# Expert weights in 4 MB transfers with 32 KB runs instead of 2 MB halves with 16 KB runs

## The chip, the cores and the metric

The kernel runs on one core of a Trainium2 chip. The metric is the device time of one execution in microseconds (us). Three executions of the kernel before took 2572.22 to 2574.54 us, median 2573.12 us.

## What is computed

The reference runs two blocks one after the other on 512 tokens of 1024 float32 features. The first (a recurrent layer, a pooling layer and their dense feed-forward parts) is not touched by the change. The second has two layers (`l` = 0, 1), each an attention part and then a mixture of experts, cut here to what matters:

```python
aff = jax.nn.softmax(logits, axis=-1)              # 512 tokens x 16 experts
gate, idx = lax.top_k(aff.transpose(0, 2, 1), 64)  # each expert takes 64 tokens
xs = x[bidx, idx]
hid = jax.nn.silu(xs @ w_gate) * (xs @ w_up)       # per expert, 64 x 1024
ys = (hid @ w_down) * gate
return jnp.zeros_like(x).at[bidx, idx].add(ys)
```

`w_gate`, `w_up` and `w_down` are 1024 x 1024 float32 for each of 16 experts, so 4 MB a matrix, 48 matrices or 201 MB a layer.

## The kernel before, in words

Everything is placed by hand in one SBUF array, `arena`, and every engine has its own instruction stream with semaphore waits written out.

**Slots.** The weights of the experts go through a ring of 11 slots of 16 KB per partition (`ring2`, each 2 MB in all). A matrix is loaded as two halves of 512 rows. Partition p of a half holds rows 4p to 4p+3, which are contiguous in memory: one run of 16 KB per partition (`load`, L476 to L499, the transfer itself at L493 for most halves). The halves are numbered n = 0 to 95 in the order of their use. Two experts make a pair: halves 12i to 12i+11 are gate and up of expert 2i, gate and up of expert 2i+1, and then the first halves of both w_down and the second halves of both. Half n goes to slot `ORDER[n % 11]`, so the load of half n waits until half n - 11 was used. The first eleven wait instead for the end of whatever lay in their slot before. Half 11 goes in two pieces (L488, L489). SyncE's queue issues all of these in order, and each load stands behind the wait of the one ahead of it. The last four halves are cut finer: L495 loads their first 8 KB per partition, L503 (`load_rest`) the rest, the very last ones by columns.

**TensorE**, for each expert: `inner` (matmuls at L2711) multiplies the 64 gathered tokens by gate and then by up, 16 matmuls of 512 columns for each half matrix; two column halves of the result run side by side on the two 64-column halves of the array, one for weight columns 0 to 511, one for 512 to 1023. Then four transposes of `hid` (L2790). After the second expert of a pair, `outer` (L2745) multiplies both experts' hidden rows by their two w_down matrices, side by side: first with both first halves, then, after a further wait, with both second halves. Between these lie the matmuls that add the previous pair's result into the tokens (`scattered`, L2756) and the transposes of the next pair's gathered tokens (L2696; for the first two experts L2684). In the last pair `outer_last` (L2729) and `scattered_last` (L2763) do the same in finer steps.

A transposed token chunk must have the rows that the weights have: as partition p holds rows 4p to 4p+3 of a half, the transposes read every fourth feature (L2684, L2696), and the layer's norm gain is brought in the same order (`gperm`).

**GpSimdE** gathers the tokens of each next pair from memory by an indirect transfer (128 rows of 4 KB), issued once the previous gathered tokens have been transposed.

After layer 0 the same SyncE queue goes on with layer 1's input weights (`w_in`, L463), which wait for slots of the ring, and with `w_out` (L511).

Of the kernel before, what the change touches and what calls it, by code (L numbers as in the profile page):

```python
# [19 lines left out]
D = 1024  # L20
# [71 lines left out]
def program(nc, a, out):  # L92
    with ExitStack() as ctx:
# [54 lines left out]

        ring2 = [at(lo, SLOT) for lo in (0, 4096, 8192, 12288, 16384, 20480, 41472, 28672, 45568, 32768, 50176)]
        x_tok = at(24576, 4096, "p (t d) -> p t d", t=TC)  # L150
# [195 lines left out]
        R2_LANDS = (3, 2, 2, 1, 1, 2, 0, 0, 0, 0, 1)  # L346
        ORDER = (10, 2, 1, 4, 3, 8, 7, 5, 0, 6, 9)
        LOADS = 6 * EXPERTS

        def loads_before(s, n):  # L350
            return sum(1 for i in range(n) if ORDER[i % 11] == s)

        def expert_load(l, n):
            s = ORDER[n % 11]
            k = loads_before(s, n)
            total = slot_total(s)
            twice = total - loads_before(s, LOADS)
            late = twice if k else 0
            return s, l * total + k + late, l * total + k + 1 + twice, 16 * (l * (R2_LANDS[s] + total) + R2_LANDS[s] + k + 1 + late)

        def slot_total(s):
            return loads_before(s, LOADS) + (1 if s == ORDER[0] else 0)

        def load_number(e, part):
            i, par = divmod(e, 2)
            return 12 * i + (4 * par + part if part < 4 else 8 + 2 * (part - 4) + par)

        def part_used(l, e, part):
            s, _, done, _ = expert_load(l, load_number(e, part))
            return r2_used[s], done  # L370

        def part_in(l, e, part):
            s, _, _, landed_at = expert_load(l, load_number(e, part))
            return s, landed_at

# [4 lines left out]
        def _(sp):  # L380
# [69 lines left out]
            for l in range(DEPTH):  # L450
# [4 lines left out]
                for s in ((10, 3, 1, 0, 4, 2), (0, 10, 4, 2, 1, 3))[l]:  # L455
                    c0, n = {0: (1152, 416), 1: (0, 384), 2: (384, 384), 3: (768, 384), 4: (1568, 384), 10: (1952, 384)}[s]
                    if l:
                        sp.wait_ge(r2_used[s], slot_total(s))
# [10 lines left out]
                def load(n):  # L469

                    i, j = divmod(n, 12)
                    e, part = (2 * i + j // 4, j % 4) if j < 8 else (2 * i + j % 2, j // 2)
                    s, free, _, _ = expert_load(l, n)
                    if n >= 11:
                        sp.wait_ge(r2_used[s], free - 1 if n == 11 else free)
                    else:  # L476
                        name, value = {10: ("conv_ps", 6 * l + 6), 0: ("wout_ps", 24 * l + 24), 1: ("q_ps", 3 * l + 3), 2: ("p2_ps", 16 * l + 16),
                                       3: ("o_ps", 18 * l + 18), 4: ("sc_done", 12 * l + 12), 5: ("wout_ps", 24 * l + 16),
                                       6: ("lgp_ps", 4 * l + 4), 7: ("wout_ps", 24 * l + 8),
                                       8: ("t_ps", 2 * l + 2), 9: ("xn_saved", 64 * l + 64)}[s]  # L480
                        sp.wait_ge(sm[name], value)
                        if s == 9:
                            sp.wait_ge(got[0], 16 * (8 * l + 1))
                    w = a[("w_gate_2", "w_up_2", "w_down_2")[part // 2]][l, e]
                    half = w[512 * (part % 2):512 * (part % 2) + 512, :]
                    if n == 11:
                        for k in (0, 2):
                            sp.wait_ge(r2_used[s], free - 1 + k // 2)  # L488
                            sp.dma_start(ring2[s].rearrange("p (k n) -> p k n", k=4)[:, k:k + 2],  # L489
                                         half.rearrange("(p k) n -> p k n", k=4)[:, k:k + 2]).then_inc(r2_in[s], 16)  # L490
                        return
                    if n < LOADS - 4:
                        sp.dma_start(ring2[s], half.rearrange("(p k) n -> p (k n)", k=4)).then_inc(r2_in[s], 16)  # L493
                        return
                    sp.dma_start(ring2[s][:, 0:2048].rearrange("p (k n) -> p k n", k=2),  # L495
                                 half.rearrange("(p k) n -> p k n", k=4)[:, 0:2]).then_inc(r2_in[s], 16)

                def load_rest(n, landed, lo, hi):

                    s = expert_load(l, n)[0]  # L500
                    q = (n - LOADS + 4) // 2
                    half = a["w_down_2"][l, EXPERTS - 2 + n % 2][512 * q:512 * q + 512, :]
                    sp.dma_start(ring2[s][:, 2048:].rearrange("p (k n) -> p k n", k=2)[:, :, lo:hi],  # L503
                                 half.rearrange("(p k) n -> p k n", k=4)[:, 2:4, lo:hi]).then_inc(landed, 16)

                if l:
                    sp.wait_ge(r2_used[5], loads_before(5, LOADS))
                else:
                    sp.wait_ge(sm["f2_ps"], F2_BASE[1] + 28)
# [6 lines left out]
                for n in (LOADS - 4, LOADS - 3):  # L516
                    load(n)
                for par in range(2):
                    load_rest(LOADS - 4 + par, r1_in[2 + par], 0, D)
                for n in (LOADS - 2, LOADS - 1):  # L520
                    load(n)
                for par in range(2):
                    load_rest(LOADS - 2 + par, r1_in[par], 0, 512)
                for par in range(2):
                    load_rest(LOADS - 2 + par, last_cols_in[par], 512, D)
            for half in range(2):
# [1393 lines left out]
        def _(pe):  # L1920
# [397 lines left out]
            for l in range(DEPTH):  # L2318
# [42 lines left out]
                def landed(s, n):  # L2361

                    pe.wait_ge(r2_in[s], 16 * (l * (R2_LANDS[s] + slot_total(s)) + n))
                    return ring2[s]
# [311 lines left out]
                def gathered(e):  # L2676
# [4 lines left out]
                    for k in range(KC):  # L2681
                        q, kk = divmod(k, 4)
                        src = xg[e][:, 512 * q:512 * q + 512].rearrange("c (p k) -> c k p", k=4)[:, kk, :]
                        ins = tr(ps[:, 4, CAP * k:CAP * k + CAP], src, ident[CAP * e:CAP * e + CAP, CAP * e:CAP * e + CAP])  # L2684
                    ins.then_inc(sm["xst_ps"], 1)

                def gathered_pair(i, q):
# [6 lines left out]
                    for kk in range(4):  # L2694
                        src = xg_pair[:, 512 * q:512 * q + 512].rearrange("c (p k) -> c k p", k=4)[:, kk, :]
                        ins = tr(ps[:, 4, P * kk:P * kk + P], src, ident)  # L2696
                    ins.then_inc(sm["xst_ps"], 1)

                def piece(e, part):

                    s, landed_at = part_in(l, e, part)
                    pe.wait_ge(r2_in[s], landed_at)
# [102 lines left out]
        def _(pool):  # L2805
# [20 lines left out]
            def second_tables():  # L2826
                for l in range(DEPTH):
# [151 lines left out]
```

## Time and profile before

| | us |
|---|---|
| median of three runs | 2573.12 |
| the profiled execution, its own time | 2574.44 |
| its span in the trace | 2572.6 |
| TensorE busy | 2474.2 (96% of the span) |
| VectorE busy | 1156.5 (45%) |
| SyncE's DMA queue (169072 packets, 544.59 MB) | 54.8% of 16 engines' span |

Times in the trace count from the start of the span. The expert stage of layer 0 lies at 1362.87 to 1807 us (first matmul of expert 0 to the end of L2763), that of layer 1 at 2124.56 to 2569 us. "Idle before" in a row is the time in which the engine did nothing ahead of that row, with what ended it.

### The profile page before, as it was taken

What the parts mean: (1) busy time and instruction counts of PE and PEld (TensorE: products, weight loads), DVE (VectorE), ACT (ScalarE), POOL (GpSimd) and SP (SyncE); (2) the same over time, 40 slices, a digit from 0 to 9 for tenths busy, and PEclk for the clock granted to TensorE, in tenths of its full rate; (3) what the DMA queues carried; (4) which work ended last, traced back from release to release, by engine and by line L of the source; (5) the groups of instructions that cost most, each with busy time, mean ns of one, the idle gap of its engine ahead of it and who ended that gap; (6) DMA issues with size and microseconds to landing.
All of it is one profiled execution on the core that took longest, in us unless ns stands there. A gap on an engine that the chain in (4) does not pass through costs nothing.

```text
span 2572.6 us, 26560 instructions
## 1 busy us (share of the span) xinstructions
PE 2474.2 (96%) x10783; PEld 1499.2 (58%) x10783; DVE 1156.5 (45%) x2015; ACT 476.9 (19%) x1009; POOL 141.7 (6%) x237
## 2 busy tenths in 40 slices
PE   7999999999999999999999999889999999999889
PEld 4458888888888888555653333333556653333333
DVE  4677888655756644324741122111334641222112
ACT  2432121002222101233710000000224610000000
POOL 1321110000000000001010000000001000000000
PEclk9999999999999999999999999999999999999999
DMA  8635774551344225202158999999421259999998
GB/s 308 210 109 180 262 245 148 155 147 34 132 130 131 66 66 156 107 24 107 40 219 359 427 427 427 427 428 419 164 93 38 76 196 411 427 427 427 427 428 350
DMA packets 187097, 601.77 MB, mean 234 GB/s; under 512 B 8960, under 2 KB 123328, under 8 KB 161632
## 3 DMA queue, kind: packets, MB, share of 16 engines
q1 hardware_dynamic: 169072, 544.59, 54.8%
q0 software_dynamic: 16608, 51.22, 5.9%
q10 hardware_dynamic: 1296, 4.25, 0.4%
q8 instruction: 87, 1.43, 0.2%
q14 instruction: 34, 0.28, 0.0%
HBM read 593.74 MB, written 6.29 MB: 233 GB/s over the span
## 4 chain that ended last, share of the span: by engine, by line
PE 78%; DMA 13%; DVE 6%; issue 1%; SPq 1%; ACT 1%; another core or an unknown queue 0%; DVEq 0%; ACTq 0%
PE ps L2711 10%; DMA arena<-in_w_down 10%; PE ps L2142 9%; PE ps L2267 7%; PE ps L2745 7%; PE ps L2379 5%; PE ps L2153 5%; PE ps L2615 4%; PE ps L2113 3%; PE ps L2373 3%; PE ps L2178 2%; PE ps L2038 2%; PE ps L2756 2%; PE ps L2060 2%; PE ps L2393 2%; DMA arena<-in_w_up 2%
## 5 line engine op out<-in xcount | busy, mean ns | idle before, releaser
L2142 PE MATMUL ps<-arena 128*128 128x256 f32 x1280 | 278.3, 380 | 2.6 <-issue 2.0
L2142 PEld LDWEIGHTS ps<-arena 128*128 128x128 f32 x1280 | 242.4, 190 | 37.2 <-issue 4.6
L2711 PE MATMUL ps<-arena,first 128*64 128x512 f32 x1024 | 231.5, 594 | 13.3 <-DMA arena<-in_w_up 12.6
L2711 PE MATMUL ps<-arena 128*64 128x512 f32 x1024 | 232.1, 594 | 2.5 <-DMA arena<-in_w_up 2.5
L2745 PE MATMUL ps<-arena 128*64 128x512 f32 x896 | 206.7, 619 | 22.6 <-DMA arena<-in_w_down 21.2
L2267 PE MATMUL ps<-arena 128*128 128x256 f32 x896 | 193.8, 379 | 0.2 <-DVE arena L1530 0.2
L2267 PEld LDWEIGHTS ps<-arena 128*128 128x128 f32 x896 | 170.1, 190 | 23.6 <-issue 0.5
L2711 PEld LDWEIGHTS ps<-arena,first 128*64 128x64 f32 x1024 | 73.3, 137 | 163.1 <-issue 136.2
L2745 PEld LDWEIGHTS ps<-arena 128*64 128x64 f32 x896 | 67.9, 142 | 158.5 <-issue 156.8
L2711 PEld LDWEIGHTS ps<-arena 128*64 128x64 f32 x1024 | 73.9, 137 | 140.2 <-issue 133.2
L2153 PE MATMUL ps<-arena 128*128 128x256 f32 x672 | 147.9, 382 | 3.4 <-DVE arena L1359 3.4
L2153 PEld LDWEIGHTS ps<-arena 128*128 128x128 f32 x672 | 128.6, 192 | 21.5 <-DVE arena L1359 3.8
L1904 DVE TENSOR_SCALAR arena<-ps,arena 128x512 f32<-128x512 f32 x32 | 22.7, 747 | 238.8 <-PE ps L2745 213.9
L2379 PE MATMUL ps<-arena 128*128 128x512 f32 x288 | 124.8, 593 | 0.0
L1880 DVE SCALAR_TENSOR_TENSOR arena<-arena,ps 128x512 f32<-128x512 f32 x32 | 22.0, 687 | 223.7 <-ACT arena L943 223.7
L2615 PE MATMUL ps<-arena 128*128 128x512 f32 x256 | 115.3, 598 | 0.0
L2113 PE MATMUL ps<-arena 128*128 128x256 f32 x512 | 112.4, 379 | 0.0
L1882 DVE SCALAR_TENSOR_TENSOR arena<-arena,ps 128x512 f32<-128x512 f32 x32 | 22.0, 688 | 199.4 <-PE ps L2711 199.4
L943 ACT ACTIVATE arena<-ps 128x512 f32<-128x512 f32 x32 | 19.1, 597 | 498.4 <-PE ps L2711 498.4
L2113 PEld LDWEIGHTS ps<-arena 128*128 128x128 f32 x512 | 97.0, 190 | 13.5 <-issue 0.5
L2756 PE MATMUL ps<-arena 128*128 128x512 f32 x224 | 104.7, 600 | 0.0
L1866 DVE TENSOR_TENSOR arena<-ps,arena 128x512 f32<-128x512 f32 x112 | 77.5, 692 | 40.8 <-PE ps L2756 40.8
(465 smaller groups left out, 3174.2 us busy)
## 6 DMA issues: line engine op xcount, KB each, us to landing
arena<-in_w_gate SPq DMA_DIRECT2D x64, 2048.0 KB, 36.5
arena<-in_w_up SPq DMA_DIRECT2D x64, 2048.0 KB, 35.3
arena<-in_w_down SPq DMA_DIRECT2D x54, 2048.0 KB, 34.4
arena<-in_ffn_w SPq DMA_DIRECT2D x24, 2048.0 KB, 9.2
arena<-in_w_mod POOLq DMA_DIRECT2D x80, 512.0 KB, 5.1
arena<-in_ffn_w SPq DMA_DIRECT2D x32, 1024.0 KB, 7.9
arena<-in_w_down SPq DMA_DIRECT2D x16, 1024.0 KB, 37.0
arena<-in_w_in SPq DMA_DIRECT2D x10, 1536.0 KB, 11.7
```

The lines of the kernel that those rows point to most:

```text
L1866: V.tensor_tensor(x, ps[:, MO_BANK[n % 4], :], x, add).then_inc(sm["mo_added"], 1)
L2038: ins = mm(ps[:, c % 2, :], w[:, k, P * (c % 4):P * (c % 4) + P], hT[:, k, :], start=(k == 0), stop=(k == KC - 1))
L2113: ins = mm(ps[:, 2 * (i % 2) + k // 4, 0:256], w[:, k, P * (i % 4):P * (i % 4) + P], hT[:, k, 0:256], start=(k % 4 == 0), stop=(k % 4 == 3))
L2142: ins = mm(ps[:, i % 6, 0:256], src[:, k, P * j:P * j + P], x[:, k, :], start=(k == 0), stop=(k == 3))
L2153: ins = mm(ps[:, F2A_BANK[n], 0:256], w[:, f, :], x[:, f, :], start=(f == 0), stop=(f == 15))
L2267: ins = mm(ps[:, bank, 0:256], w[:, f, :], x[:, f, :], start=(f == 0), stop=(f == 15))
L2373: ins = mm(out_ps, hnT[:, k, cols:cols + out_ps.shape[0]], w[:, k, :], start=(k == 0), stop=(k == KC - 1))
L2379: ins = mm(ps[:, bank, :], w[:, k, c0:c0 + P], hnT[:, k, :], start=(k == 0), stop=(k == KC - 1))
L2615: ins = mm(ps[:, OUT_BANK[n], :], mixT(k)[:, P * t:P * t + P], w[:, (k + 2) % 8 % 4, 512 * half:512 * half + 512], start=(k == ks[0]), sto ...
L2711: ins = mm(ps[CAP * half:CAP * half + CAP, bank, :], xsT[q][:, k, CAP * (e % 2):CAP * (e % 2) + CAP], wv[:, k, 512 * half:512 * half + 512 ...
L2745: ins.append(mm(ps[CAP * par:CAP * par + CAP, YE_BANK[half], :], hT2[par][:, k, CAP * q:CAP * q + CAP], w[par][0][:, k, 512 * half:512 * h ...
L2756: mm(ps[:, MO_BANK[n % 4], :], oh[:, P * t:P * t + P], ye[half], start=True, stop=True).then_inc(sm["mo_ps"], 1)
```

## The change

From matrix 7 to matrix 41 of a layer (of 48, counted m = 0 to 47 in order of use: gate, up, gate, up, down, down of each pair), all but matrix 9 come by one 4 MB transfer each (`load_whole`). A whole matrix lands in two slots that lie side by side in `arena`, partition p holding rows 8p to 8p+7 in one run of 32 KB. The other 14 matrices still come in halves, but a half is now half of each partition's eight rows (a run of 16 KB out of 32 KB). That gives 34 whole transfers per layer in the place of 68.

The ring is laid out anew: five pairs of slots, `PAIRS`, in turn. Slot 10 is used by halves 0 and 11 only; from half 12 on the ring has ten slots. The first eleven halves are issued slot by slot in the order in which slots come free (`FREED`), as before, but which half goes to which slot is set by `FIRST`. A whole load waits for both of its slots; a reader of either half waits for the whole matrix. Matrix m takes the slots of matrix m - 5 (m from 11 on); matrices 6 to 10 take the slots of the halves in `FIRST`.

So that one partition can hold eight rows, the transposes of the gathered tokens read every eighth feature, the gain is brought as eight in a row, and the two column halves of `inner` are no longer columns 0 to 511 and 512 to 1023, but the first and the last four of each eight columns, which gives `hid` and its transposes the same place as the rows of w_down.

```diff
-        ORDER = (10, 2, 1, 4, 3, 8, 7, 5, 0, 6, 9)
-        LOADS = 6 * EXPERTS
+        MATS = 3 * EXPERTS
+        FREED = (10, 2, 1, 4, 3, 8, 7, 5, 0, 6, 9)
+        FIRST = (10, 6, 8, 7, 9, 0, 1, 2, 3, 4, 5, 10)
+        PAIRS = ((6, 8), (7, 9), (0, 1), (2, 3), (4, 5))
+
+        def half_slot(m, q):
+            return FIRST[2 * m + q] if m < 6 else PAIRS[(m - 6) % 5][q]
+
+        def is_whole(m):
+            return 7 <= m < MATS - 6 and m != 9
+
+        def land_slot(m, q):
+            return half_slot(m, 0 if is_whole(m) else q)
...
+                def slot_free(m, q):
+
+                    s = half_slot(m, q)
+                    sp.wait_ge(r2_used[s], l * use_total(s) + use_count(s, m, q) - 1)
...
+                def load_half(m, q):
+
+                    s = half_slot(m, q)
+                    slot_free(m, q)
+                    sp.dma_start(ring2[s], matrix(m)[:, SLOT * q:SLOT * q + SLOT]).then_inc(r2_in[s], 16)
+
+                def load_whole(m):
+
+                    s = half_slot(m, 0)
+                    slot_free(m, 0)
+                    slot_free(m, 1)
+                    sp.dma_start(at(RING2_AT[s], 2 * SLOT), matrix(m)).then_inc(r2_in[s], 16)
...
-                for n in range(LOADS - 4):
-                    load(n)
+                for s in FREED:
+                    load_first(FIRST.index(s))
+                load_eleventh()
+                for q in range(2):
+                    load_half(6, q)
+                for m in range(7, MATS - 2):
+                    if is_whole(m):
+                        load_whole(m)
+                    else:
+                        for q in range(2):
+                            load_half(m, q)
...
-                        q, kk = divmod(k, 4)
-                        src = xg[e][:, 512 * q:512 * q + 512].rearrange("c (p k) -> c k p", k=4)[:, kk, :]
+                        src = xg[e].rearrange("c (p k) -> c k p", k=KC)[:, k, :]
...
-                        src = xg_pair[:, 512 * q:512 * q + 512].rearrange("c (p k) -> c k p", k=4)[:, kk, :]
+                        src = xg_pair.rearrange("c (p k) -> c k p", k=KC)[:, 4 * q + kk, :]
...
-                                ins = mm(ps[CAP * half:CAP * half + CAP, bank, :], xsT[q][:, k, CAP * (e % 2):CAP * (e % 2) + CAP], wv[:, k, 512 * half:512 * half + 512],
+                                ins = mm(ps[CAP * half:CAP * half + CAP, bank, :].rearrange("c (n j) -> c n j", j=4),
+                                         xsT[q][:, k, CAP * (e % 2):CAP * (e % 2) + CAP],
+                                         wv[:, k, :].rearrange("p (n j) -> p n j", j=KC)[:, :, 4 * half:4 * half + 4],
                                          start=(q == 0 and k == 0), stop=(q == 1 and k == 3))
...
-                    pool.dma_start(gperm[:, l, :].rearrange("p (q k) -> p q k", q=2),
-                                   a["norm_ffn_2"][l].rearrange("(q p k) -> p q k", q=2, k=4)).then_inc(sm["gains_in"], 16)
+                    pool.dma_start(gperm[:, l, :], a["norm_ffn_2"][l].rearrange("(p k) -> p k", k=KC)).then_inc(sm["gains_in"], 16)
```

The last pair (matrices 42 to 47) keeps its loads by halves and its finer pieces at the end.

## Rows read from the trace of the kernel before

**Rows 1.** The page, part 2: rate of all DMA in 40 slices.
```profile
GB/s 308 210 109 180 262 245 148 155 147 34 132 130 131 66 66 156 107 24 107 40 219 359 427 427 427 427 428 419 164 93 38 76 196 411 427 427 427 427 428 350
```
**Rows 2.** Stretches of layer 0's expert stage: stretch, length, busy times, clock, DMA share, GB/s.
```profile
1500.00:1600.00 100.00, 97.98 (x433) 35.26 (x434) 20.68 (x31) 4.78 (x8) 2.29 (x4) 1.00 1.01 427
1600.00:1700.00 100.00, 85.20 (x365) 31.79 (x362) 18.84 (x28) 3.58 (x6) 2.29 (x4) 0.98 1.01 428
```
**Rows 3.** Who waited for whom over the span, TensorE: total us, times, longest.
```profile
PE ps L2745 <- DMA arena<-in_w_down: 21.2, 6, 4.0
PE ps L2711 <- DMA arena<-in_w_up: 15.2, 15, 1.6
```
**Rows 4.** TensorE in order of time (start, us, work), pairs 1 and 2.
```profile
1451.56 13.95 PE L2745 MATMUL ps<-arena 128*64 128x512 f32 x64
1465.35 3.60 PE L2711 MATMUL ps<-arena 128*64 128x512 f32 x16
...
1503.48 13.95 PE L2745 MATMUL ps<-arena 128*64 128x512 f32 x64
```
**Rows 5.** TensorE in order of time, pairs 6 and 7 of layer 0.
```profile
1729.13 7.09 PE L2745 MATMUL ps<-arena 128*64 128x512 f32 x32
1738.90 8.78 PE L2745 MATMUL ps<-arena 128*64 128x512 f32 x32 [2.68 <-DMA arena<-in_w_down]
1747.49 3.63 PE L2711 MATMUL ps<-arena 128*64 128x512 f32 x16
...
1758.39 3.65 PE L2711 MATMUL ps<-arena,first 128*64 128x512 f32 x16 [0.41 <-DMA arena<-in_w_up]
...
1777.98 3.65 PE L2711 MATMUL ps<-arena,first 128*64 128x512 f32 x16 [1.25 <-DMA arena<-in_w_up]
...
1792.99 7.36 PE L2729 MATMUL ps<-arena 128*64 128x512 f32 x32 [0.24 <-DMA arena<-in_w_down]
```
**Rows 6.** The chain of waits in order of time, layer 0's end.
```profile
1692.39 46.38 DMA arena<-in_w_down
...
1755.94 36.91 DMA arena<-in_w_down
```
**Rows 7.** All DMA from 1440 to 1740 us, then from 1776.6 to 1786.4 us.
```profile
DMA packets 9330, 128.09 MB, mean 427 GB/s; under 512 B 1032, under 2 KB 1032, under 8 KB 1672
```
```profile
DMA packets 564, 4.14 MB, mean 422 GB/s; under 512 B 63, under 2 KB 63, under 8 KB 63
```
**Rows 8.** SyncE's queue in order of time: issues of halves 11, then 14 and 15.
```profile
1364.89 2.00 SPq L489 DMA_DIRECT2D arena<-in_w_down  x2
...
1376.86 6.67 SPq L493 DMA_DIRECT2D arena<-in_w_up  x2
```
**Rows 9.** Issue to landing, us: half 8 (issued 1336.7), half 29 (issued 1441.9).
```profile
arena<-in_w_down SPq DMA_DIRECT2D x1, 2048.0 KB, 7.4
```
```profile
arena<-in_w_gate SPq DMA_DIRECT2D x1, 2048.0 KB, 25.8
```
**Rows 10.** A stretch of TensorE after the wait of 2.68 us; columns as in rows 2.
```profile
1738.90:1742.30 3.40, 3.40 (x10) 1.26 (x12) 0.00 (x0) 0.00 (x0) 0.00 (x0) 0.59 1.01 429
```
**Rows 11.** TensorE by line and form: busy us, mean ns, idle before.
```profile
L2455 PE MATMUL ps<-tbl,const 120*64 120x192 f32 x64 | 5.6, 329 | 0.0
```
```profile
L2545 PE MATMUL ps<-arena 128*128 128x192 f32 x48 | 9.8, 326 | 0.0
```
```profile
L2696 PEld LDWEIGHTS ps<-const,arena 128*128 128x128 f32 x112 | 16.5, 207 | 19.0 <-issue 17.0 <-DVE arena L1855 1.9
...
L2336 PEld LDWEIGHTS ps<-const,arena 128*128 128x128 f32 x64 | 7.5, 140 | 5.5 <-issue 4.2 <-DVE arena L1720 1.3
```
**Rows 12.** TensorE in order of time, pairs 6 and 7 of layer 1.
```profile
2500.47 8.78 PE L2745 MATMUL ps<-arena 128*64 128x512 f32 x32 [2.69 <-DMA arena<-in_w_down]
2509.06 3.63 PE L2711 MATMUL ps<-arena 128*64 128x512 f32 x16
...
2554.55 7.13 PE L2729 MATMUL ps<-arena 128*64 128x512 f32 x32 [0.23 <-DMA arena<-in_w_down]
```

More of the change, by code:

```diff
@@ L145, in program @@
         tiny = sb("tiny", [P, 1])
-        ring2 = [at(lo, SLOT) for lo in (0, 4096, 8192, 12288, 16384, 20480, 41472, 28672, 45568, 32768, 50176)]
+        RING2_AT = (0, 4096, 8192, 12288, 16384, 20480, 41472, 28672, 45568, 32768, 50176)
+        ring2 = [at(lo, SLOT) for lo in RING2_AT]
         x_tok = at(24576, 4096, "p (t d) -> p t d", t=TC)
@@ L346, in program @@
         R2_LANDS = (3, 2, 2, 1, 1, 2, 0, 0, 0, 0, 1)
-        ORDER = (10, 2, 1, 4, 3, 8, 7, 5, 0, 6, 9)
-        LOADS = 6 * EXPERTS
[L350 to L359, printed above, removed]
@@ new lines, in land_slot, with land_count, use_count @@
+        def land_slot(m, q):
+            return half_slot(m, 0 if is_whole(m) else q)
+        def land_count(s, m, q):
+            n = 0
+            for i in range(2 * m + q + 1):
+                mm, qq = divmod(i, 2)
+                if land_slot(mm, qq) == s and not (is_whole(mm) and qq):
+                    n += 2 if i == 11 else 1
+            return n
+        def use_count(s, m, q):
+            return sum(2 if i == 0 else 1 for i in range(2 * m + q + 1) if half_slot(*divmod(i, 2)) == s)
@@ L365, in load_number, with land_total, use_total, half_of @@
+        def land_total(s):
+            return land_count(s, MATS - 1, 1)
+        def use_total(s):
+            return use_count(s, MATS - 1, 1)
+        def half_of(e, part):
             i, par = divmod(e, 2)
-            return 12 * i + (4 * par + part if part < 4 else 8 + 2 * (part - 4) + par)
+            return 6 * i + (2 * par + part // 2 if part < 4 else 4 + par), part % 2
         def part_used(l, e, part):
-            s, _, done, _ = expert_load(l, load_number(e, part))
-            return r2_used[s], done
+            m, q = half_of(e, part)
+            s = half_slot(m, q)
+            return r2_used[s], l * use_total(s) + use_count(s, m, q)
@@ L372, in part_in @@
         def part_in(l, e, part):
-            s, _, _, landed_at = expert_load(l, load_number(e, part))
-            return s, landed_at
+            m, q = half_of(e, part)
+            s = land_slot(m, q)
+            return half_slot(m, q), r2_in[s], 16 * (l * (R2_LANDS[s] + land_total(s)) + R2_LANDS[s] + land_count(s, m, q))
         block = ctx.enter_context(nc.Block())
@@ L457, in _ @@
                     if l:
-                        sp.wait_ge(r2_used[s], slot_total(s))
+                        sp.wait_ge(r2_used[s], use_total(s))
                     elif s < 10:
@@ L467, in _ @@
                         sp.dma_start(ring2[s][:, 3072:3648], uq[:, s - 1, :]).then_inc(r2_in[s], 16)
[L469 to L504, printed above, removed]
+                def matrix(m):
+                    i, j = divmod(m, 6)
+                    w = a[("w_gate_2", "w_up_2")[j % 2] if j < 4 else "w_down_2"][l, 2 * i + (j // 2 if j < 4 else j - 4)]
+                    return w.rearrange("(p k) n -> p (k n)", k=KC)
@@ new lines, in slot_free, with load_first @@
+                def slot_free(m, q):
+                    s = half_slot(m, q)
+                    sp.wait_ge(r2_used[s], l * use_total(s) + use_count(s, m, q) - 1)
+                def load_first(n):
+                    m, q = divmod(n, 2)
+                    s = FIRST[n]
+                    name, value = {10: ("conv_ps", 6 * l + 6), 0: ("wout_ps", 24 * l + 24), 1: ("q_ps", 3 * l + 3), 2: ("p2_ps", 16 * l + 16),
+                                   3: ("o_ps", 18 * l + 18), 4: ("sc_done", 12 * l + 12), 5: ("wout_ps", 24 * l + 16),
+                                   6: ("lgp_ps", 4 * l + 4), 7: ("wout_ps", 24 * l + 8),
+                                   8: ("t_ps", 2 * l + 2), 9: ("xn_saved", 64 * l + 64)}[s]
+                    sp.wait_ge(sm[name], value)
+                    if s == 9:
+                        sp.wait_ge(got[0], 16 * (8 * l + 1))
+                    sp.dma_start(ring2[s], matrix(m)[:, SLOT * q:SLOT * q + SLOT]).then_inc(r2_in[s], 16)
@@ new lines, in load_eleventh @@
+                def load_eleventh():
+                    s = FIRST[11]
+                    for k in range(2):
+                        sp.wait_ge(r2_used[s], l * use_total(s) + 1 + k)
+                        sp.dma_start(ring2[s][:, 2048 * k:2048 * k + 2048], matrix(5)[:, SLOT + 2048 * k:SLOT + 2048 * k + 2048]).then_inc(r2_in[s], 16)
+                def load_half(m, q):
+                    s = half_slot(m, q)
+                    slot_free(m, q)
+                    sp.dma_start(ring2[s], matrix(m)[:, SLOT * q:SLOT * q + SLOT]).then_inc(r2_in[s], 16)
@@ new lines, in load_whole, with load_last @@
+                def load_whole(m):
[3 more added lines that the diff above has]
+                    sp.dma_start(at(RING2_AT[s], 2 * SLOT), matrix(m)).then_inc(r2_in[s], 16)
+                def load_last(par, q):
+                    s = half_slot(MATS - 2 + par, q)
+                    slot_free(MATS - 2 + par, q)
+                    sp.dma_start(ring2[s][:, 0:2048], matrix(MATS - 2 + par)[:, SLOT * q:SLOT * q + 2048]).then_inc(r2_in[s], 16)
@@ L506, in _, with load_rest @@
+                def load_rest(par, q, landed, lo, hi):
+                    s = half_slot(MATS - 2 + par, q)
+                    w = matrix(MATS - 2 + par)[:, SLOT * q + 2048:SLOT * q + SLOT].rearrange("p (k n) -> p k n", k=2)
+                    sp.dma_start(ring2[s][:, 2048:].rearrange("p (k n) -> p k n", k=2)[:, :, lo:hi], w[:, :, lo:hi]).then_inc(landed, 16)
                 if l:
-                    sp.wait_ge(r2_used[5], loads_before(5, LOADS))
+                    sp.wait_ge(r2_used[5], use_total(5))
@@ L513, in _ @@
                 sp.dma_start(ring2[0].rearrange("p (k n) -> p k n", k=4), w_out[:, 2:6, :]).then_inc(r2_in[0], 16)
-                for n in range(LOADS - 4):
-                    load(n)
-                for n in (LOADS - 4, LOADS - 3):
-                    load(n)
+                for s in FREED:
[9 more added lines that the diff above has]
+                            load_half(m, q)
                 for par in range(2):
-                    load_rest(LOADS - 4 + par, r1_in[2 + par], 0, D)
-                for n in (LOADS - 2, LOADS - 1):
-                    load(n)
+                    load_last(par, 0)
                 for par in range(2):
-                    load_rest(LOADS - 2 + par, r1_in[par], 0, 512)
+                    load_rest(par, 0, r1_in[2 + par], 0, D)
                 for par in range(2):
-                    load_rest(LOADS - 2 + par, last_cols_in[par], 512, D)
+                    load_last(par, 1)
+                for par in range(2):
+                    load_rest(par, 1, r1_in[par], 0, 512)
+                for par in range(2):
+                    load_rest(par, 1, last_cols_in[par], 512, D)
             for half in range(2):
@@ L2361, in landed @@
                 def landed(s, n):
[L2363 removed]
+                    pe.wait_ge(r2_in[s], 16 * (l * (R2_LANDS[s] + land_total(s)) + n))
                     return ring2[s]
@@ L2699, in piece @@
                 def piece(e, part):
-                    s, landed_at = part_in(l, e, part)
-                    pe.wait_ge(r2_in[s], landed_at)
+                    s, landed, landed_at = part_in(l, e, part)
+                    pe.wait_ge(landed, landed_at)
                     return ring2[s].rearrange("p (k n) -> p k n", k=4), r2_used[s]
```

3 lines of the change are left out of this document (removed).

## The prediction, made before the changed kernel was run

> **What bounds the kernel now.** I read the page first. TensorE is busy 96% of the span, which suggests that a DMA change can bring nothing. The slices say otherwise: twice, for five slices and more, all DMA moves 427 to 428 GB/s and nothing higher anywhere [rows 1]. These are the two expert stages. A layer's 201.3 MB at 427.5 GB/s take 471 us. So I cut layer 0's stage into stretches: TensorE is 98% busy from 1500 to 1600 us and only 85% from 1600 to 1700, at the same DMA rate [rows 2]. In the first part TensorE works off what was loaded ahead, in the second it waits for weights. The waits name the loads: 21.2 us for w_down, 15.2 us for up, over both layers [rows 3].
>
> The two rates, per pair of experts: without waits TensorE needs 1503.48 - 1451.56 = 51.9 us [rows 4]. DMA needs 12 halves of 2.097 MB / 427.5 GB/s = 4.9 us, or 58.9 us, and 1.2 us more for a gather (0.52 MB). DMA is the slower by 7 to 8 us a pair. The chain of waits agrees: it goes through the load that ends at 1692.39 + 46.38 = 1738.77, then TensorE and queue pieces, then the load that ends at 1792.85 [rows 6]. But TensorE is close behind. In the last pair of layer 0 the waits are 0.41, 1.25 and 0.24 us, 1.9 in all [rows 5]. Hence the question is not only how fast the weights come, but at what moment TensorE may begin on them.
>
> **Part 1, longer runs.** What a packet costs beyond its bytes is read from the two sizes the trace has: 427 GB/s in the stretch of 16 KB packets (gathers included) and 422 GB/s where the pieces have 8 KB per partition [rows 7]. 2.097 MB take 4.91 and 4.97 us; the 0.06 us are the price of doubling the packets of 2 MB (8 more and one more completion on each of 16 engines). A 4 MB transfer in 32 KB runs saves just that number against two halves, so 0.06 us. Times 34 whole matrices: 2.0 us a layer by the last whole one. Ends: nothing, if a 32 KB run is cut up again; 3.4 us, if the difference is 0.10 us, as a rate 9 GB/s lower would give. I take 2.0, from the row itself.
>
> The Trainium skill (SBUF — State Buffer, "The DMA setup-cost knee") gives each transfer about 2 us beside its bytes and asks for the largest single transfer. By it 34 transfers fewer would be 68 us a layer. The rows show 2 MB transfers side by side at 427 GB/s, with no such gap, as several are under way at once.
>
> **Part 2, the queue at the start.** Half 12 onwards has ten slots, not eleven, and a whole load waits for two. Did DMA run dry? Loads of halves 14 and 15 went out at 1376.9 and 1376.86 + 6.67 - 0.33 = 1383.2 [rows 8]. The whole matrix 7 needs the slot that is used up at the latter moment, so it goes out at 1383.2; half 13 and the first gather keep DMA busy until about then, and an idle queue needs 7.4 - 4.9 = 2.5 us before bytes count [rows 9]. Further on the narrowest place is matrix 15: it takes the slots of w_down matrix 10, free at the end of `outer` at 1465.35 [rows 4]. What was asked for before it ends with half 29, which lands at 1441.9 + 25.8 = 1467.7 [rows 9], some 0.5 us sooner with the whole matrices before it. A load issued at 1465.4 lands 7.4 + 4.9 = 12.3 us later, at 1477.7, where an unbroken stream would give 1467.2 + 9.8 = 1477.0: 0.7 us lost. After that TensorE gains on nothing (51.9 against 59 us), and the queue stays full. Ends: 0, and 2.5 us for one start from an idle queue. I take 0.7.
>
> **Part 3, where w_down is waited for.** This is the costly part. Before, `outer` of pair 6 began at 1729.13 with both first halves and only its second part waited, until 1738.90 [rows 5]: half of `outer`'s work lay beside the last load. Now both w_down matrices must be whole, and the whole of it follows that load. The DMA before stays the bound up to there, so earlier pairs hide the shift: `outer` starts at the landing, work for the pair ends 51.9 us later, the next landing is 59 us later. The last pair does not hide it. Its own loads are by halves and their stream ends as before, but TensorE enters it later:
> - landing of matrix 41, by TensorE's start: 1738.90 - 2.0 + 0.7 = 1737.6;
> - `outer` unbroken: 1465.35 - 1451.56 = 13.8 us [rows 4], to 1751.4 (before: 1747.49);
> - the last pair up to the second part of L2729: 1792.99 - 1747.49 = 45.5 us, less the 1.9 us of waits, 43.6 us, to 1795.0.
>
> Against 1792.99 that is 2.0 us. Everything behind it (L2729, L2763, layer 1) moves along.
>
> **Part 4, the clock.** The wait ahead of `outer` is now one piece: 59 - 52, some 5 to 7 us, where before it was 2.7 to 4.0 us. After the wait of 2.68 us the granted clock was 0.59 in the next 3.4 us [rows 10], the 1.2 GHz level for most of it, and 32 matmul records took 8.78 in place of 7.09 us [rows 5], so 1.7 us more. The kernel before paid this already, and it is in 1747.49. The unbroken 13.8 us are at full clock, so the fall is to be added again: 1.7 us if it comes while TensorE works. Ends: 0 (it falls and recovers during the wait) and twice that, 3.4. I take 1.7: waits twice as long hardly pass unpunished. In earlier pairs it is covered by the slack of 7 us.
>
> The Trainium skill (TensorE: Matmul & The Clock Gate, "HAM oscillation — how this bites in real kernels") describes just this: waits on DMA between groups of matmuls throttle each next group. The trace agrees (0.59 after 2.68 us). By it every pair would start slow.
>
> **Part 5, strides.** `inner` now reads 16 bytes of every 32. The nearest row for a moving operand read in pieces is L2455, in runs of 32 bytes: 329 ns against 326 ns for a plain one of 192 columns [rows 11]; I cost it at 0. The other end is the weight load at a step of 16 bytes, 207 against 140 ns [rows 11]: 0.5 ns a step, 128 steps a matmul; per pair 64 matmuls, two side by side, so 2.1 us. For two passes over the data it is 4.2 us. The transposes at a step of 32 instead of 16 bytes lie outside the last pair's path except some twenty at the start: 0, at most 1 us.
>
> **Part 6, SyncE's queue and the rest.** 34 issues less, at 0.33 us on a queue that waits anyway: 0. Layer 1's w_in stand behind the same last loads and find their slots free no later than before: 0. The gain transfer is early: 0. A gather's packets now alternate with packets twice as long, so a gather lands some microseconds later, but has a pair's time (the first one has about 3 us of room): 0.
>
> **Sum.** Layer 0: -2.0 + 0.7 + (13.8 - 8.6 for the part of `outer` after the landing) - 1.9 of waits that vanish + 1.7 = +3.7 us, where 8.6 is 1747.49 - 1738.90. Layer 1 has the same rows: 2500.47 - 1.3 + 13.8 + (45.49 - 1.9) + 1.7 = 2558.3 against 2554.55 [rows 12], again +3.7. Together +7.4 us on the profiled 2574.44, which is 1.3 over the median; on the median, 2580.5 us.
>
> **Rivals.** What a measurement of this kernel can tell from no change is about 0.2%, 5.1 us.
> - *The tail is a draw.* The clock does not fall at work, packets save 3.4 us: 1737.6 - 1.4 + 13.8 + 43.6 = 1793.6, +0.6 a layer, 2574.3. For it: the waits of 3.96 us elsewhere cost nothing at times. Chance 0.25.
> - *The columns in fours are slow.* +4.2 us in each last pair, on top: 2580.5 + 8.4 = 2588.9. It decides from about 1 us a pair on; under 7 us the earlier pairs hide it. Only L2455 speaks against it. 0.10.
> - *Faster: the end stays with DMA.* If `outer` and the last pair had room that I miss (its w_down pieces still wait at the end), the landings set the end, at -2.0 + 0.7, or with 3.4 us saved -3.4 a layer: 2570.5 to 2566.3. It decides where TensorE's part after matrix 41 falls under 54 us; rows 5 make it 57.4. 0.07. The 2 us a transfer of the Trainium skill (same page and section as above) would add to this side; I give it 0.01 of these.
>
> **Numbers.** Forecast 0.58, 2576 to 2585; a fifth of it lies within 5.1 us. Slower: 0.58 x 0.8 + 0.10 + a little of the draw = 0.59. Faster by more than 0.2%: 0.05. Same: 0.36. The range goes from 2572.5 to 2588: below, the draw; above, no saving, 2.5 us lost and a double fall give (2.0 + 1.8 + 1.7) x 2 = 11 us more than forecast, of which I take most.
>
> **What would show it.** Right: L2745 waits for w_down before its first matmul in four pairs of each layer, 4 to 7 us each, about 45 us in place of 21.2; no wait at L2711 and L2729 in the last pair; some 177300 packets in place of 187097 (68 x 144 less), middle slices at 429 or 430 GB/s; L2711 still 594 ns; the start of the second part of L2729 3 to 4 us later than before, counted from the first L2711. Wrong: a wait for DMA left at L2729, packets not fewer, L2711 over 600 ns, or landings before `outer` of pair 6 over 3 us earlier.

## The result, and the profile after

The changed kernel took 2580.94 us, median of seven runs (2579.31 to 2588.56), against 2574.54 us for the kernel before, also seven runs (2572.22 to 2576.24). The ratio is 1.003, with a 95% interval of 1.0021 to 1.0039: slower by 0.2 to 0.4%, some 5 to 10 us. The forecast was 2580.5 us. It stood on a median before of 2573.12 us, so as a change it was +7.4 us; measured were +6.4 us by the medians and +7.7 us by the ratio. That the two times agree to 0.4 us is luck, that the changes agree to about 1 us is not.

Lines moved down: `inner` is now L2755, `outer` L2791, `outer_last` L2775, `scattered` L2802, `scattered_last` L2809 and the transposes of gathered pairs L2740. First the page of the kernel after, part 2 and the packets:

```profile
GB/s 298 205 118 177 264 245 147 155 146 38 134 122 130 65 66 175 86 52 79 67 197 382 422 434 430 429 430 412 117 98 33 98 189 408 418 430 434 429 428 320
DMA packets 177306, 601.76 MB, mean 233 GB/s; under 512 B 7873, under 2 KB 122241, under 8 KB 160545
```

The middle slices of both expert stages went from 427 or 428 [rows 1] to 428 to 434 GB/s, and 9791 packets are gone: the 32 KB runs are real and not cut up. But the first full slice of each stage, 427 and 411 before, now has 422 and 408, and the one behind it in layer 1 went from 427 to 418. The waits of TensorE on expert weights, over the whole span:

```profile
PE ps L2791 <- DMA arena<-in_w_down: 43.3, 8, 6.8
...
PE ps L2755 <- DMA arena<-in_w_up: 1.1, 2, 0.8
```

Before, 21.2 us of waits in 6 places stood in `outer`, ahead of one of its parts, and 15.2 us were strewn over `inner` [rows 3]. Now nearly all is ahead of `outer`, once for each of four pairs a layer, 4.1 to 6.8 us each. The end of layer 0 in order of time (start, us, work; in square brackets the idle time ahead):

```profile
1741.37 15.88 PE L2791 MATMUL ps<-arena 128*64 128x512 f32 x64 [6.16 <-DMA arena<-in_w_down]
1757.06 3.61 PE L2755 MATMUL ps<-arena 128*64 128x512 f32 x16
...
1785.36 3.60 PE L2755 MATMUL ps<-arena,first 128*64 128x512 f32 x16
...
1792.99 13.95 PE L2775 MATMUL ps<-arena 128*64 128x512 f32 x64
1806.88 7.13 PE L2809 MATMUL ps<-arena 128*128 128x512 f32 x16
```

This is what rows 5 became. `outer` is one block of 64 records behind one wait. (The trace has two records for each float32 matmul that the kernel issues: the loops of `outer` issue 32, those of `inner` 8 for a half matrix, where the description above counts 16.) From 1757.06 to the end there is not one wait for weights: TensorE, not DMA, now sets the end of the stage. The granted clock of the first 3.4 us of that block (stretch, length, busy times, clock, DMA share, GB/s):

```profile
1741.40:1744.80 3.40, 3.40 (x8) 1.06 (x10) 0.00 (x0) 0.00 (x0) 0.00 (x0) 0.50 0.97 414
```

A granted clock of 0.50 is the 1.2 GHz level; before it was 0.59 at the same place [rows 10]. All eight blocks that waited in the changed kernel took 15.4 to 16.6 us, where one at full clock takes 13.95.

The whole spans of two profiles differ by up to 5.5 us for reasons outside the expert stages. One of them is TensorE's clock, which falls at a few other moments in some executions and not in others: a block of 32 records in layer 1's attention took 10.57 us before at a granted clock of 1.00, and 12.26 us in the changed kernel, where it was 0.86 from 1952.7 to 1965 us. The profiled execution of the changed kernel was its slowest of seven (2588.56 us). So from here on I measure inside the stage, from the first matmul of `inner` to the first of `scattered_last`. The table puts all kernels side by side, in us from the stage's start; the runs e1 to e8 are told below. "Landing" is the moment at which the last work of `outer` of pair 6 that waited for w_down began; where `outer` did not wait, none is given.

| kernel | layer 0: landing | layer 0: `outer` of pair 6 ends | layer 0: end | layer 1: end | both stages | ratio to before (95%) |
|---|---|---|---|---|---|---|
| before | 376.03 | 384.62 | 437.41 | 437.05 | 874.46 | |
| changed | 376.32 | 392.01 | 441.83 | 441.40 | 883.23 | 1.0030 (1.0021 to 1.0039) |
| e1 | 375.81 | 391.98 | 441.80 | 441.67 | 883.47 | 1.0036 (1.0023 to 1.0050) |
| e2 | - | 382.32 | 436.12 | 436.90 | 873.02 | 0.9999 (0.9990 to 1.0008) |
| e3 | 376.59 | 385.17 | 437.92 | 438.13 | 876.05 | 1.0009 (1.0000 to 1.0018) |
| e4 | 376.21 | 392.21 | 442.02 | 444.24 | 886.26 | 1.0052 (1.0038 to 1.0066) |
| e5 | 375.38 | 389.13 | 438.97 | 439.22 | 878.19 | 1.0011 (1.0002 to 1.0019) |
| e6 | 375.53 | 382.41 | 436.96 | 436.61 | 873.57 | 0.9994 (0.9986 to 1.0003) |
| e7 | 374.09 | 389.26 | 439.07 | 439.05 | 878.12 | 1.0019 (1.0010 to 1.0028) |
| e8 | - | 383.02 | 436.15 | 435.29 | 871.44 | 0.9988 (0.9980 to 0.9997) |

The changed kernel lost 4.4 us in each stage, 8.8 us in all. The ratio, over seven executions of each, says 7.7 us.

Each row of the table is one profile. How far to trust a landing, e1 and e3 tell: their loads are the same up to matrix 39, and their landings differ by 0.8 us (0.9 in layer 1). The landings of layer 1 are 375.91 us before, 376.34 in the changed kernel, 376.17 in e1, 377.05 in e3, 378.01 in e4, 375.63 in e5, 375.41 in e6 and 374.15 in e7.

### The profile page after: what moved, and what is told of

Read it like the earlier page. It is cut to its first block, busy times and chain, and to the rows that moved or that the text cites. A ratio compares the mean times of both kernels' runs of the same rounds, so it can differ in the third digit from the quotient of the medians.

```text
span 2586.8 us, 26558 instructions
## 1 busy us (share of the span) xinstructions
PE 2479.8 (96%) x10783; PEld 1503.6 (58%) x10783; DVE 1155.9 (45%) x2015; ACT 476.9 (18%) x1009; POOL 141.4 (5%) x237
## 4 chain that ended last, share of the span: by engine, by line
PE 80%; DMA 13%; DVE 5%; issue 1%; ACT 1%; SPq 0%; DVEq 0%; ACTq 0%
DMA arena<-in_w_down 11%; PE ps L2755 11%; PE ps L2187 9%; PE ps L2791 8%; PE ps L2312 7%; PE ps L2424 5%; PE ps L2198 5%; PE ps L2660 4%; PE ps L2158 3%; PE ps L2418 3%; PE ps L2223 2%; PE ps L2083 2%; PE ps L2105 2%; PE ps L2438 2%; PE ps L2802 2%; PE ps L2595 1%
## 5 line engine op out<-in xcount | busy, mean ns | idle before, releaser
L2791 PE MATMUL ps<-arena 128*64 128x512 f32 x896 | 213.3, 638 | 44.6 <-DMA arena<-in_w_down 43.3
L2755 PE MATMUL ps<-arena 128*64 128x512 f32 x1024 | 232.0, 594 | 1.1 <-DMA arena<-in_w_up 1.1
L2755 PE MATMUL ps<-arena,first 128*64 128x512 f32 x1024 | 230.8, 592 | 0.0
L2791 PEld LDWEIGHTS ps<-arena 128*64 128x64 f32 x896 | 71.6, 147 | 184.1 <-issue 182.3
L2755 PEld LDWEIGHTS ps<-arena,first 128*64 128x64 f32 x1024 | 75.2, 137 | 144.5 <-issue 144.5
L2755 PEld LDWEIGHTS ps<-arena 128*64 128x64 f32 x1024 | 73.5, 137 | 139.0 <-issue 133.7
L2802 PE MATMUL ps<-arena 128*128 128x512 f32 x224 | 104.7, 600 | 0.0
```

The costliest lines, as they stand in the source:

```text
L2755: ins = mm(ps[CAP * half:CAP * half + CAP, bank, :].rearrange("c (n j) -> c n j", j=4), xsT[q][:, k, CAP * (e % 2):CAP * (e % 2) + CAP], w ...
L2791: ins.append(mm(ps[CAP * par:CAP * par + CAP, YE_BANK[half], :], hT2[par][:, k, CAP * q:CAP * q + CAP], w[par][0][:, k, 512 * half:512 * h ...
L2802: mm(ps[:, MO_BANK[n % 4], :], oh[:, P * t:P * t + P], ye[half], start=True, stop=True).then_inc(sm["mo_ps"], 1)
```

## The experiments

All eight start from the changed kernel. In some, w_down goes back to halves in the old alternating order; for that the loop in SyncE's queue has this branch:

```diff
                     if is_whole(m):
                         load_whole(m)
-                    else:
+                    elif m % 6 == 4:
+                        for q in range(2):
+                            for par in range(2):
+                                load_half(m + par, q)
+                    elif m % 6 < 4:
                         for q in range(2):
                             load_half(m, q)
```

**e1: only the last two w_down come whole.** Two whole transfers a layer are left of 34, the two that pair 6's `outer` reads.

```diff
-            return 7 <= m < MATS - 6 and m != 9
+            return m in (MATS - 8, MATS - 7)
```

> The changed kernel, but of each layer only the two w_down matrices of pair 6 (40 and 41) come whole; all others by halves, w_down in the old alternating order. Theory (the cost is that outer of pair 6 starts only when both matrices are whole, and the last pair cannot hide it): landing as before, outer 13.8 us after it instead of 8.6, and the last pair's 1.9 us of waits gone, so 3.3 us a layer later, or 5.0 with a clock fall; no saving, as only 2 transfers change. 6 to 10 us over the kernel before, about 2582 us. Rival (the loss comes from the queue running dry on whole loads early in a layer, or is spread over all pairs): within 2 us of before.

Measured: 2584.5 us, ratio 1.0036, so 9 us over before and about as slow as the full change. Its layer 0, in order of time:

```profile
1739.49 16.35 PE L2795 MATMUL ps<-arena 128*64 128x512 f32 x64 [9.59 <-DMA arena<-in_w_down]
...
1791.59 13.95 PE L2779 MATMUL ps<-arena 128*64 128x512 f32 x64
```

The landing is where it was before (375.81 against 376.03), and the stage still ends 4.4 us later. e1 also has the new rows and the new ring, and the kernel with just these is e3. Against e3 the two transfers at this one place cost 3.9 and 3.5 us, 7.4 of the 8.8 us, and 7 us by the ratios. The rival, that an early dry spell or a loss spread over all pairs makes the loss, is out: this kernel has neither (428 GB/s from 1376 to 1476 us). One thing is not separated. In all these kernels, w_down by halves also means another order of the four halves (both first ones, then both second ones) and a wait for each. No run loads the halves in the order of the whole matrices with a wait for each, so it is open how much of the late start that order alone would make.

**e2: everything whole but these two.** The complement of e1.

```diff
-            return 7 <= m < MATS - 6 and m != 9
+            return 7 <= m < MATS - 8 and m != 9
```

> The changed kernel, but the two w_down matrices of pair 6 come by halves in the old alternating order; 32 matrices a layer still come whole. Theory: outer of pair 6 starts on the first halves again, the end is set by DMA once more and the saving of packets shows up: landing of the last w_down half 0.3 us later than before as measured from the first expert matmul, so 0 to +1 us over the kernel before, 2573 to 2576 us, 5 to 7 us under the changed kernel. Rival (spread over all pairs, or clock falls in each pair): still over 2579 us.

Measured: 2575.31 us, ratio 0.9999. The loss is gone with 32 of 34 whole transfers still in place. `outer` of pair 6 did not wait at all, and DMA sets the end again, as the last wait shows:

```profile
1731.96 13.95 PE L2795 MATMUL ps<-arena 128*64 128x512 f32 x64
...
1757.35 3.65 PE L2759 MATMUL ps<-arena,first 128*64 128x512 f32 x16 [1.13 <-DMA arena<-in_w_up]
...
1792.28 7.34 PE L2779 MATMUL ps<-arena 128*64 128x512 f32 x32 [0.24 <-DMA arena<-in_w_down]
```

**e6: two pairs in the middle.** Only w_down of pairs 3 and 4 whole, four transfers a layer.

```diff
-            return 7 <= m < MATS - 6 and m != 9
+            return m in (22, 23, 28, 29)
```

> As the kernel with halves only, but the w_down matrices of pairs 3 and 4 (22, 23, 28, 29) come whole, twice as many as in the run in which only pair 6's did. Theory (a later start of outer is hidden by the slack of 7 us a pair up to the next landing): the time of the kernel with halves only within 2 us, about 2576 us, with waits ahead of outer of pairs 3 and 4. Rival (each whole w_down costs 3 to 5 us wherever it stands): over 2587 us.

Measured: 2574.84 us, ratio 0.9994. The trace has the longer waits and the clock falls, and neither reaches the end:

```profile
1559.93 15.65 PE L2795 MATMUL ps<-arena 128*64 128x512 f32 x64 [4.03 <-DMA arena<-in_w_down]
...
1620.11 16.93 PE L2795 MATMUL ps<-arena 128*64 128x512 f32 x64 [6.54 <-DMA arena<-in_w_down]
```

Those blocks take 1.7 and 3.0 us more than at full clock (13.95), and the stages are no longer than before. The same edit costs 3.5 to 3.9 us a layer at pair 6 (e1 against e3) and nothing that shows at pairs 3 and 4. Against the kernel with halves only (e3) it is even 2.2 us faster by the medians, just outside the 2 us that I had given, and 3.9 us by the ratios, which set each against its own measurement of the kernel before. The intervals overlap, and the cause is open. The traces have one difference that shows what sets the end: after the same wait of 2.7 us the second part of pair 6's `outer` took 7.09 us here in layer 0 and 8.78 us in e3, so with the earlier landing `outer` ended 2.8 us earlier, but the stage only 1.0 us earlier. Where DMA sets the end, most of what TensorE gains goes into waits.

**e3: no whole transfer.** New rows, column groups, steps of eight and ten slots, but halves throughout.

```diff
-            return 7 <= m < MATS - 6 and m != 9
+            return False
```

> The changed kernel with no whole transfers at all: halves in the old alternating order, but the new rows (8p to 8p+7), column groups of four, transposes at a step of eight, ten slots and the new first eleven. Theory: strides and slots cost nothing, so the time of the kernel before within 0.1% (2572 to 2577 us), L2755 at 594 ns. Rival (columns in fours or the ring cost something that the whole transfers pay back): over 2579 us.

Measured: 2577.03 us, the very edge of what was expected, ratio 1.0009 (1.0000 to 1.0018). The matmuls on columns in fours:

```profile
L2759 PE MATMUL ps<-arena 128*64 128x512 f32 x1024 | 232.1, 595 | 0.1
L2759 PE MATMUL ps<-arena,first 128*64 128x512 f32 x1024 | 231.5, 594 | 14.8 <-DMA arena<-in_w_up 14.8
```

594 and 595 ns are the 594 of before, to the nanosecond or so. The grouping is free. What the rest (ten slots, another order at the start) costs is 0 to 4.6 us by the ratio and 1.6 us by the stages. The forecast had it at 0, and which part of it costs something, if any does, is open.

**e4: the same waits, two 2 MB transfers at once.** This takes the long runs away and leaves the waits and the order as they are. It also makes 34 transfers a layer more, so it prices the two together.

```diff
-                    sp.dma_start(at(RING2_AT[s], 2 * SLOT), matrix(m)).then_inc(r2_in[s], 16)
+                    for q in range(2):
+                        sp.dma_start(at(RING2_AT[s] + SLOT * q, SLOT), matrix(m)[:, SLOT * q:SLOT * q + SLOT]).then_inc(r2_in[s], 16)
```

`land_count` counts two arrivals for such a matrix.

> The changed kernel with the same waits for slots and for whole matrices, but each of the 34 whole loads issued as two transfers of 2 MB in runs of 16 KB, one right behind the other. It isolates the packets. Theory: 0.06 us a matrix, 2 us a layer, all of it ahead of the last pair: 4 us over the changed kernel, about 2585 us, and 427 to 428 GB/s in the middle instead of 429 to 431. Rival (the rate does not depend on the run): the changed kernel's time within 1 us.

Measured: 2588.28 us, ratio 1.0052, 5.7 us more than the changed kernel's ratio gives, where 4 was expected; 3.0 us by the stages. The rate from 1496 to 1596 us is 427 GB/s in e4 and 432 in the changed kernel. Over the longer stretches of both layers (1500 to 1720 and 2240 to 2460 us) it is 427 against 430. So fewer transfers with longer runs do raise the rate. In time, 5.7 us has an interval of about 1.4 to 10 us, which leaves the "no change" rival (within 1 us) just outside. In layer 0 alone the landing is the same in both (376.21 and 376.32), in layer 1 it is 1.7 us later (378.01 against 376.34), so a single profile does not settle the size per layer. Whether it is the run or the number of transfers that counts, no run tells.

**e5: TensorE kept busy in the wait.** Twelve more matmuls on constants ahead of the last unbroken `outer`.

```diff
                         if i < EXPERTS // 2 - 1:
+                            if i == EXPERTS // 2 - 2:
+                                awake(12)
                             outer(i)
```

> The changed kernel with 12 more matmuls of 256 columns on constants, about 5.3 us, ahead of outer of pair 6 in each layer, where TensorE otherwise waits 5 to 6 us for w_down. Their result is overwritten and unused. Theory (the clock fall is part of the price): outer of pair 6 takes 13.9 us instead of 15.4 to 15.9, and the kernel ends 3 to 4 us before the changed one, about 2577 us. Rival (the fall costs nothing at the end, or other falls take its place): the changed kernel's time within 1.5 us; or later by up to 2 us, if the extra matmuls outlast the wait.

Measured: 2579.62 us, ratio 1.0011, by the ratios 4.9 us under the changed kernel (about 1.6 to 8). The twelve matmuls are the x24 of the first row:

```profile
1733.30 5.34 PE L2699 MATMUL ps<-const 128*128 128x256 f32 x24
1740.49 13.95 PE L2791 MATMUL ps<-arena 128*64 128x512 f32 x64 [1.85 <-DMA arena<-in_w_down]
1754.24 3.63 PE L2755 MATMUL ps<-arena 128*64 128x512 f32 x16
```

`outer` takes 13.95 us instead of 15.88, and the granted clock of its first 3.4 us is 1.00 in both layers. The stages are 5.0 us shorter in all; 1.9 and 1.5 us of it are the blocks themselves, the rest is that their landings came 0.9 and 0.7 us sooner in this profile, within the scatter of landings between kernels. The price of the clock fall is real and about as forecast.

**e7: whole transfers from matrix 16 on.** This tests the dry spell at the start.

```diff
-            return 7 <= m < MATS - 6 and m != 9
+            return 16 <= m < MATS - 6
```

> The changed kernel with whole transfers from matrix 16 on (26 a layer instead of 34), so that DMA is ahead of TensorE when they begin. Theory (DMA ran dry around matrix 15, some 2 us a layer, when whole loads began at 7): landing ahead of outer of pair 6 about 1 to 1.5 us earlier from the first expert matmul, 2 to 3 us under the changed kernel, about 2578.5 us. Rival (the dry spell is the same or made up by the packets): the changed kernel's time within 1 us.

Measured: 2580.88 us, with 2576.32 us for the kernel before in the same comparison, ratio 1.0019, 2.8 us under the changed kernel by the ratios. The two intervals overlap, so the times alone don't show the gain; the traces do. Two stretches near the start, first of the changed kernel, then of e7:

```profile
1376.00:1476.00 100.00, 95.65 (x432) 34.88 (x430) 18.30 (x28) 4.78 (x8) 3.47 (x6) 0.98 1.00 421
1466.00:1476.00 10.00, 10.00 (x50) 3.34 (x48) 2.10 (x3) 0.60 (x1) 0.00 (x0) 1.00 0.94 378
```
```profile
1376.00:1476.00 100.00, 95.66 (x440) 35.16 (x438) 18.27 (x28) 4.78 (x8) 3.47 (x6) 1.00 1.01 427
1466.00:1476.00 10.00, 10.00 (x50) 3.38 (x48) 0.69 (x1) 0.60 (x1) 0.00 (x0) 1.00 1.01 428
```

421 against 427 GB/s over 100 us is 1.4 us of DMA time lost, most of it (1.2 us) in the ten microseconds in which matrix 15 waits for the end of `outer`. With eight whole transfers fewer, the landing ahead of pair 6's `outer` is 2.2 us earlier in both layers (374.09 against 376.32, 374.15 against 376.34).

But the depth of the dry spell is not a matter of the loads alone. `outer` of the first pair takes 13.95 us in some stages and 15.3 to 15.7 in others, a clock fall that comes in the kernel before too, and with it `outer` of the second pair, whose slots matrix 15 needs, starts 1.5 to 2.1 us later in the stage. (Load 15 went out 102.6 us into layer 0's stage in the changed kernel and 100.9 us in e2.) In the ten microseconds from 101 to 111 us of the stage, the four kernels whose whole loads begin at 7 (changed, e2, e4, e5) moved 360 to 380 GB/s in their six stages with that fall and 405 and 411 in the two without (layer 0 of e2 and of e4). The other kernels moved 424 to 434 with the fall or without. So the dry spell comes from whole loads that begin early. It is 0.4 to 0.5 us of DMA time without the early clock fall and 1.1 to 1.6 us with it; no run forced that fall, so its share is read from eight stages and not from an edit. The changed kernel's profile had the fall in both layers and e7's in neither, so these two profiles together overstate what beginning later gains. The row of e2 beside the 378 of the changed kernel:

```profile
1466.00:1476.00 10.00, 10.00 (x48) 3.30 (x46) 0.69 (x1) 0.60 (x1) 0.00 (x0) 1.00 0.99 418
```

**e8: both mended.** Whole transfers for matrices 16 to 39, w_down of pair 6 by halves.

```diff
-            return 7 <= m < MATS - 6 and m != 9
+            return 16 <= m < MATS - 8
```

> Both mended: whole transfers for matrices 16 to 39 only, w_down of pair 6 by halves. Theory: DMA sets the end, 24 whole matrices save 1.4 us a layer and nothing is lost early, so 2 to 3 us under the kernel before, about 2572 us on its median of 2574.5. Rival (nothing of the saving reaches the end, as the landings did not come earlier in the changed kernel): the time of the kernel before within 1 us.

Measured: 2573.78 us against 2576.32 in the same comparison, ratio 0.9988 (0.9980 to 0.9997): 3 us faster than the kernel before by the ratio, 1 to 5 us by its interval. The stages agree: 871.44 against 874.46 us. DMA is again the one that sets the end, so the saving of packets can arrive there:

```profile
1734.25 13.95 PE L2795 MATMUL ps<-arena 128*64 128x512 f32 x64
...
1793.94 7.29 PE L2779 MATMUL ps<-arena 128*64 128x512 f32 x32 [0.32 <-DMA arena<-in_w_down]
```

How much of the 3 us it is, is open: e6, with four whole matrices a layer, stands at 0.9994 and e2, with 32, at 0.9999, and the three intervals overlap.

## Why the prediction was right, step by step

- **What bounds.** Right: DMA sets the pace, TensorE is 7 to 8 us a pair ahead of it, and the last pair has some 2 us of waits. e1, e2 and e6 show each part: the same late start of `outer` costs 3.5 to 3.9 us a layer (e1 against e3) where no later wait can absorb it, and nothing that shows where one can.
- **Part 1, longer runs** (0.06 us a matrix). About right: 430 GB/s instead of 427 over the two stretches of 220 us is 0.07 us for 4 MB; the 432 from 1496 to 1596 us, which would be 0.11 us, is one stretch. e4 puts a price of 3 us (stages) to 5.7 us (ratios) on both layers, where the term was 4. There is luck in it: the term came from ten microseconds at 422 GB/s, and stretches of ten microseconds scatter by more than that (424 to 434 GB/s at one place in the stages of the kernels that ran without a dry spell).
- **Part 2, the dry start** (0.7 us). This is the term most off. The place was right, matrix 15 behind `outer`, but 1.2 us were lost there and 1.4 us over the first 100 us, and because of this the landing was not 1.3 us earlier, as summed, but 0.3 us later (e5, with the same loads, had it 0.7 and 0.3 us earlier). The step that was off is how long the loads already asked for would keep DMA busy: to 1467.2 us, 104.3 us into the stage, by the sum. In the changed kernel the rate was 197 GB/s in the microsecond from 1467 us, 102 us into the stage, before load 15 had gone out. The rows of the sum had the early clock fall that e7 tells of, so 0.7 stands against the 1.1 to 1.6 us of the stages with it.
- **Part 3, `outer` after the landing** (13.8 us, and 1.9 us of waits that vanish). With the clock included `outer` ended 15.7 us after the landing, where 15.5 were forecast. From there to the first matmul of `scattered_last` it was 1806.88 - 1757.06 = 49.8 us, and before 1800.28 - 1747.49 = 52.8 us, so 3.0 us went and not 1.9 (2.7 us in layer 1). The idle time in a row understates a wait: from 1754.35 to 1758.39 is 4.04 us, against 3.43 for the same block without a wait, so a wait listed with 0.41 us held up 0.6.
- **Part 4, the clock** (1.7 us). 15.69 - 13.79 = 1.9 us in layer 0 and 1.5 us in layer 1; e5 took it away. In the middle it costs up to 3.0 us a block (e6) and is hidden. All eight blocks behind a wait were slow in the changed kernel. Before, one of the two parts that had waited 3.96 us ran at full clock (7.09 us, from 1618.59 us, granted clock 1.00) and the other did not (8.78 us, from 1680.14 us), so a wait of about 4 us does not always bring the fall.
- **Part 5, strides** (0). Right: 592 to 595 ns in every kernel.
- **Part 6.** SyncE's shorter list and layer 1's w_in changed nothing that the traces show. The gathers did land later, and were never waited for in a pair. A wait of 1.4 us for expert 0's gather, ahead of layer 1's stage, occurs in the changed kernel, and the same kind in e1, e3, e4 and e6 (1.2 to 2.8 us in all), but not in before, e2, e5, e7 and e8. It goes with no edit that I can name, lies ahead of the stages as measured here, and its cause is open.
- **Sum.** For layer 0, 3.7 us forecast and 4.4 measured: the landing came 1.6 us later than summed, `outer` took 0.2 more, and the tail gave back 1.1. The errors partly cancelled. One sign missed its mark a little: the middle of `outer_last`, where its second part starts, came about 4.8 us later than before (an estimate, half of the block's 13.89 us), where 3 to 4 us had been named.

## What to carry to other kernels

Merging transfers makes their reader wait for all of the merged data, so ask for each merged transfer what work lay beside its second half, and whether a later wait absorbs the shift. In a stream bound by DMA a late start in the middle was forgiven here (e6) and one just before the last user was not (e1). So merge in the middle, keep the last pieces and the ones just before them small, and begin to merge only once DMA is well ahead; e7 and e8 began at matrix 16 and had no dry spell. A stage that ends on DMA with 2 us of room for compute is bound by both.

## What was not expected of the hardware

The transposes' weight loads at a step of 32 bytes are no slower than at 16 bytes but a little faster, 193 ns against 207 [rows 11], and 193 ns in all eight further runs:

```profile
L2740 PEld LDWEIGHTS ps<-const,arena 128*128 128x128 f32 x112 | 15.5, 193 | 19.1 <-issue 17.1 <-DVE arena L1900 2.0
```

And the rate of DMA rose from 427 to 430 GB/s over 220 us with transfers of 4 MB in runs of 32 KB, and to 432 in one stretch of 100 us. A gather pays for it: its 128 rows of 4 KB landed 11.5 us after the issue before (median of 14) and 15.7 us after it in the changed kernel, 15.6 to 15.8 us in e2, e5, e7 and e8, but 10.9 to 11.6 us in e1, e3, e4 and e6, where few weights or none come in runs of 32 KB.
